# Stacked rounded queries and doubled keys for the attention scores of a two-block transformer kernel, with row sums from a column of ones

## The reference

```python
def _sliding_window_branch(q, k, v, z, sinks):
    ...
    s = jnp.einsum("bnqkgd,bnskd->bnkgqs", q, kb).astype(jnp.float32) * (SW_HD ** -0.5)
    s = jnp.where(valid[None, :, None, None], s, NEG_INF)
    ...
    p = jax.nn.softmax(jnp.concatenate([s, sink], axis=-1), axis=-1)[..., :-1]
    o = jnp.einsum("bnkgqs,bnskd->bnqkgd", p.astype(vb.dtype), vb).reshape(B, T, BRANCH_W)
    return o * jax.nn.silu(z)

def nsa_mixer(h, rel_bias, w_in, ...):
    ...   # o_cmp: attention over 15 compressed blocks
    o_sel = selected_attention(q, k_s, v_s, sel_idx, tbl, scale)   # here all 4 blocks are selected
    o_win = window_attention(q, k_w, v_w, tbl, scale)              # window 512 covers all 256 tokens
    o = gates[..., 0:1] * o_cmp + gates[..., 1:2] * o_sel + gates[..., 2:3] * o_win
    return o.reshape(B, S, H * NSA_V) @ w_o
```

## Time and profile before

| | |
|---|---|
| device time, median of 3 runs | 1417.76 us (1417.66 to 1418.02) |
| span of the profiled execution | 1415.6 us |
| median less the profiled span | 2.2 us |
| TensorE busy | 1403.6 us, 99% |
| VectorE, ScalarE, GpSimd busy | 924.5, 741.6, 65.1 us |
| share of TensorE in the chain that ended last | 94% |
| granted TensorE clock, mean | 0.999 |

### The profile page before, as it was taken

The page is one execution under the profiler, slowest core; times in us unless marked ns, Lnnn a source line. Parts: engine busy times, 40 slices in busy tenths (PEclk is TensorE's granted clock), DMA queues, the critical chain, the costliest instruction groups (busy, mean ns, idle before and its releaser), DMA issues.

```text
span 1415.6 us, 23050 instructions
## 1 busy us (share of the span) xinstructions
PE 1403.6 (99%) x8944; PEld 1270.0 (90%) x8944; DVE 924.5 (65%) x1341; ACT 741.6 (52%) x1008; POOL 65.1 (5%) x89
## 2 busy tenths in 40 slices
PE   9999999999999999999999999999999999999998
PEld 8989999999988888899888888888889999888886
DVE  5555797675566665777766666656657578666656
ACT  7556664343455445558554445544445358554454
POOL 2000010000010000010220000100000000200000
PEclk9999999999999999999999999999999999999999
DMA  8544431265545555561465554755555400555552
GB/s 325 189 146 143 168 131 60 90 209 193 179 155 201 180 197 186 174 200 59 163 260 196 187 191 166 260 186 178 188 197 184 144 31 2 185 210 184 194 191 89
DMA packets 34774, 239.69 MB, mean 169 GB/s; under 512 B 3914, under 2 KB 4058, under 8 KB 6928
## 3 DMA queue, kind: packets, MB, share of 16 engines
q1 hardware_dynamic: 32832, 231.39, 47.1%
q0 software_dynamic: 1440, 6.67, 1.5%
q10 hardware_dynamic: 432, 0.66, 0.1%
HBM read 237.10 MB, written 1.08 MB: 168 GB/s over the span
## 4 chain that ended last, share of the span: by engine, by line
PE 94%; DVE 2%; issue 1%; ACT 1%; DMA 0%; POOL 0%; POOLq 0%; ACTq 0%; DVEq 0%
PE ps L729 22%; PE ps L699 15%; PE ps L701 15%; PE ps L700 15%; PE ps L737 11%; PE ps L956 3%; PE ps L979 2%; PE ps L966 1%; PE ps L1243 1%; PE ps L2776 1%; PE ps L2784 1%; PE ps L638 1%; PE ps L2788 1%; PE ps L2952 1%; PE ps L820 1%
## 5 line engine op out<-in xcount | busy, mean ns | idle before, releaser
L406 DVE TENSOR_TENSOR low<-raw,high 128x2048 fp32r<-128x2048 f32 (+2 forms) x194 | 439.8, 2269 | 206.4 <-ACT high L400 203.9
L400 ACT ACTIVATE high<-raw 128x2048 fp32r<-128x2048 f32 (+1 forms) x197 | 372.1, 1891 | 44.8 <-PE ps L701 40.4
L729 PE MATMUL ps<-nt,high 128*128 128x512 f32 x1344 | 320.1, 390 | 0.0
L729 PEld LDWEIGHTS ps<-nt,high 128*128 128x128 f32 x1344 | 249.0, 188 | 50.7 <-issue 0.9
L699 PE MATMUL ps<-nt,high 128*128 128x256 f32 x656 | 186.0, 284 | 0.0
L701 PE MATMUL ps<-nt,low 128*128 128x256 f32 x656 | 184.8, 282 | 0.0
L700 PE MATMUL ps<-nt,high 128*128 128x256 f32 x656 | 184.8, 282 | 0.0
L737 PEld LDWEIGHTS ps<-nt,low 128*128 128x128 f32 x1344 | 167.5, 189 | 3.6
L737 PE MATMUL ps<-nt,low 128*128 128x256 f32 x1344 | 168.6, 283 | 0.0
L699 PE MATMUL ps<-high,hth 128*128 128x512 f32 x320 | 124.5, 389 | 0.0
L700 PE MATMUL ps<-low,hth 128*128 128x512 f32 x320 | 124.5, 389 | 0.0
(11 more groups left out here) (404 smaller groups left out, 2188.7 us busy)
## 6 DMA issues: line engine op xcount, KB each, us to landing
raw<-in_stream SPq DMA_DIRECT2D x215, 1024.0 KB, 4.9
late<-in_w POOLq DMA_DIRECT2D x1, 2048.0 KB, 9.4
scr<-bias_by_distance POOLq DMA_DIRECT2D x1, 2048.0 KB, 12.9
scr<-in_mem SPq DMA_DIRECT2D x2, 512.0 KB, 5.2
raw<-in_stream SPq DMA_DIRECT2D x4, 256.0 KB, 6.0
raw<-in_stream SPq DMA_DIRECT2D x2, 512.0 KB, 7.5
x<-in_x SPq DMA_DIRECT2D x1, 1024.0 KB, 8.0
con<-in_con SPq DMA_DIRECT2D x1, 592.0 KB, 8.9
```

What stands on the lines that cost most here:

```text
L400: nc.scalar.activation(high_of(t, slice(0, n)), raw[t % SLOTS][:, 0:n], ACT.Copy).then_inc(w_high, 1)
L406: nc.vector.tensor_tensor(low_of(t, slice(0, n)), raw[t % SLOTS][:, 0:n], high_of(t, slice(0, n)).bitcast(F32), ALU.subtract).then_inc(w_l ...
L729: last = nc.tensor.matmul(r3(bank, 2), w[:, k, P * j:P * j + P], nt[:, :, k, :], start=first and k == 0, stop=not first and k == KC - 1, s ...
```

## The change: what it does

**Scores of SW and NSA.** Each head's queries are stored twice over the partitions in one fp32r tensor: rounded on the 64 partitions where the head lies, the remainder on the other 64. The keys are stored on both halves, once rounded and once as remainder. One matmul over all 128 partitions then sums rounded query x key and remainder x key; the scores are two fp32r products (rounded keys, remainder keys) for each of the two token tiles, all 256 wide (L1011), in the place of f32 products 256 and 128 wide. MLA and XM keep their f32 scores. The zero-padded keys and their memsets go.

**Row sums.** The values get a 65th column of ones (a 129th for XM), so that L979's place (L1037 in the changed file) gives the row sum in PSUM. exp no longer accumulates, the mask instruction yields the scaled negative maximum directly, so the small instruction for it is gone in causal units.

**Outputs by two heads.** Reciprocal, gate and evacuation are one instruction each for two heads (256 columns). The loops run one iteration longer, and the turns of the outputs come one iteration later. The multiplication of the SW outputs by silu(z) and the addition of the NSA outputs into `late` move to GpSimd (4 and 16 instructions of 128x256), which raises `at_weighted`; `pe_turn("yc")` and the NSA turns wait for that.

**New preparation.** ScalarE makes the rounded queries and keys, VectorE the remainders; TensorE waits for `ns_low` 6 (all queries, ks and kw) ahead of NSA's first scores. Some buffers are placed elsewhere and some semaphores are merged.

The core of the diff:

```diff
+        def act_high_queries(q, j, src):
+            for own, _, heads in halves_of_heads(q, j):
+                last = nc.scalar.activation(heads[own], r3(src, 2)[own], ACT.Copy)
+            return last
+        def dve_low_queries(q, j, src):
+            for own, other, heads in halves_of_heads(q, j):
+                last = nc.vector.tensor_tensor(heads[other], r3(src, 2)[own], heads[own].bitcast(F32), ALU.subtract)
+            return last
+        def dve_low_keys(keys, n, src):
+            for (own, to, k), (_, _, high_) in zip(key_parts(keys[1], n), key_parts(keys[0], n)):
+                last = nc.vector.tensor_tensor(k[to], src[own], high_[own].bitcast(F32), ALU.subtract)
+            return last
...
+                products = u["products"]
                 for t in (1, 0):
-                    c = cols_of(u, t)
-                    last = nc.tensor.matmul(ps[a % 2][:, c], u["q"][:, P * t:P * t + P],
-                                            u["k"][:, 0:c.stop - c.start], start=True, stop=True)
+                    c = cols_of(u, t) if len(products) == 1 else slice(S - S * t, 2 * S - S * t)
+                    for n, (q, k) in enumerate(products):
+                        last = nc.tensor.matmul(ps[a % 2][:, c], q[:, P * t:P * t + P], k[:, 0:c.stop - c.start],
+                                                start=n == 0, stop=n == len(products) - 1, skip_group_check=True)
...
+                scale = q_negscale[:, t:t + 1] if u["scale"] is None else -u["scale"]
+                most = neg_sink[:, a - SW0:a - SW0 + 1] if sinks else 3e38
+                last = nc.vector.tensor_tensor_reduce(at_s[b][:, c], ps[a % 2][:, c], m, scale, most, ALU.add, ALU.min,
+                                                      at_nm[r][:, t:t + 1])
...
-            dve_step(dve, "swkv")
-            b = read_bank(dve, "swkv")
-            zeroed_here(dve, "sw_k")
-            for kv in range(SW_KV):
-                for half in range(2):
-                    nc.vector.tensor_copy(padded(sw["k"], kv, half)[64 * half:64 * half + 64],
-                                          b[64 * kv:64 * kv + 64, 0:S])
-            bank_read("swkv", nc.vector.tensor_copy(sw_vt, b[:, S:2 * S]))
             dve_turn(dve, "ym")
+            dve.wait_ge(sw_high, 3)
+            bank_read("swkv", dve_low_keys(sw_ks, SW_KV, r3(ps[bank_of("swkv")][:, 0:S], 1)))
...
             act_turn(act, "ym")
+            bank = read_bank(act, "swkv")
+            nc.scalar.activation(sw_vt, bank[:, S:2 * S], ACT.Copy)
+            act_high_keys(sw_ks, SW_KV, r3(bank[:, 0:S], 1)).then_inc(sw_high, 1)
...
+            for p in range(SW_H // 2):
+                pool.wait_ge(at_read, SW0 + 2 * p + 2)
+                yo, zo = (pair_of_heads(as3(b, TT), 2 * p, SW_D) for b in (sw["y"], sw["z"]))
+                nc.gpsimd.tensor_tensor(yo, yo, zo, ALU.mult).then_inc(at_weighted, 1)
...
+            for q in range(NSA_H):
+                pool.wait_ge(at_read, NSA0 + 2 * q + 2)
+                if q >= NSA_H // 2:
+                    pool.wait_ge(at_weighted, SW_H // 2 + q - NSA_H // 2 + 1)
+                yo = pair_of_heads(ny, 2 * q % NSA_H, NSA_D)
+                nc.gpsimd.tensor_tensor(yo, yo, ns_new(q), ALU.add).then_inc(at_weighted, 1)
...
-            pe.wait_ge(at_read, SW0 + SW_H)
+            pe.wait_ge(at_weighted, SW_H // 2)
             pe_turn(pe, "yc")
...
+            pe.wait_ge(ns_low, 6)
+            zeroed_here(pe, "nsa_ones")
```

More of the change, by code:

```diff
@@ new lines, in build, with stacked, high_low_keys @@
+        ml_v_ = [with_ones(v, 0, MLA_H, MLA_V) for v in (mls["v0"], ml["v1"])]
+        ns_v = {n: [with_ones(ns[n], t, NSA_G, NSA_D) for t in range(TT)] for n in ("vs", "vw")}
+        def stacked(q, heads):
+            return q.rearrange("p (h s) -> p h s", h=heads)
+        def high_low_keys(k, groups):
+            return [r3(k[:, S * groups * n:S * groups * n + S * groups], groups) for n in range(2)]
+        sw_qs, ns_qs = stacked(sw_queries, SW_H), stacked(ns_queries, NSA_H)
+        sw_ks = high_low_keys(sw_keys, SW_KV)
@@ L1083, in dve_units @@
                 if a < first + n:
+                    dve_scores(dve, ch, a, False)
+                ch.join()
+                if a < first + n:
+                    nc.vector.tensor_scalar(at_nm[a % RING], at_mx[a % RING], -UNITS[a]["scale"], None, ALU.mult)\
+                        .then_inc(at_max, 1)
+                if e >= first:
+                    evac(e, o, inv).then_inc(at_read, 1)
+        def dve_units(dve, ch, first, n, evac, lead, sinks=False, y=None, weigh=None, splits=()):
+            for a in range(first, first + n + 5):
+                if a == first + 2:
+                    lead()
+                p, odd = divmod(a - 4, 2)
+                ready = odd and first <= a - 4 < first + n
+                if ready:
+                    inv = at_inv[p % 3]
+                    dve.wait_ge(at_out, 2 * p + 2)
+                    sums = pair_out(p)[:, :, :, 64]
@@ L1091, in dve_units @@
-                    ins.then_inc(at_max, 1)
-                b, off = divmod(a - (first + n - 2 * KC) - 10, 4)
+                        ch.mark(nc.vector.tensor_tensor(by_unit(at_sums[p % 3]), sums, by_unit(at_sinkexp[p % 3]), ALU.add))
+                    else:
+                        ch.mark(nc.vector.reciprocal(by_unit(inv), sums))
+                if a < first + n:
+                    dve_scores(dve, ch, a, sinks)
+                if ready and sinks:
+                    ch.join()
+                    ch.mark(nc.vector.reciprocal(inv, at_sums[p % 3]))
+                elif ready and weigh:
+                    ch.join()
+                    ch.mark(weigh(p, inv))
@@ L1735, in _ @@
             ch.link(nc.gpsimd.memset(one_col, 1.0))
+            for v in xm_v + sw_v_:
+                last = nc.gpsimd.memset(v[:, :, v.shape[2] - 1:v.shape[2]], 1.0)
+            last.then_inc(zeroed, 1)
             pool.wait_ge(ident_here, 16)
@@ L2676, in _ @@
             pe_pair_tile(pe, "swz0", 1)
-            for name in ("swq0", "swq1"):
+            for name in ("swq0", "swq1", "swkv"):
                 wait_bank(pe, name)
-            pe.wait_ge(sw_v, 1)
+            pe.wait_ge(sw_high, 4)
             pe.wait_ge(turn_low, turn_done("ym"))
@@ L2917, in _ @@
             pe.wait_ge(ml_krd, 16)
+            zeroed_here(pe, "mla_ones")
             def rest_of_v():
```

395 lines of the change are left out of this document (226 added, 169 removed).

## The result

The changed kernel takes 1419.64 us in the median of 15 runs (1418.69 to 1421.83); the kernel before, run beside it, 1417.66 us (1417.40 to 1418.36). The ratio is 1.0015, 95% interval 1.0008 to 1.0021: slower by 0.15%, 2.0 us, where 1.0 us faster was forecast. The time lies inside the forecast's range and inside the 0.2% that the forecast takes as no change, but the interval excludes 1, and the sign is the opposite one. The profiled execution took 1419.13 us with a span of 1417.3, which is 1.7 more than the span of the kernel before (1415.6).

What follows compares the result with a forecast made beforehand. TensorE, busy 99% of the span, was taken to bound the kernel. The terms -7.0 + 3.7 + 1.4 + 2.4 - 1.5 = -1.0 us gave span 1414.6 and time 1416.7 against 1417.76, range 1413.4 to 1420.3.

Steps and rivals of the forecast that it cites:

- The start of NSA, +3.7 (3.0 to 3.7): Ahead of NSA's first scores TensorE idles 3.0 to 3.7 us, waiting for all of `ns_low`; 3.7 taken.
- rival (4): TensorE's clock starts slow after the stop at NSA's start, costing 1.9 to 3.0 us: 1418.6 to 1419.7; chance 0.13.
- Scores, -7.0: In 40 SW and NSA units four fp32r products take 0.176 us less than the f32 ones: -7.0 us.
- The claim that VectorE stays covered: In the SW and NSA units VectorE and ScalarE lose work, so stay covered though the unit shrinks to 1.47 us.
- the 65th column costs nothing: In the units, values growing from 64 to 65 columns are costed at nothing; 0.6 us if it cost its share.
- The way into SW, +1.4 (0.9 to 1.8): At swz0's second half TensorE waits for the bank of swkv, read late by VectorE's key remainders: 0.9 to 1.8 us.
- The end of SW, +2.4: At `pe_turn("yc")` GpSimd's silu(z) multiplication ends behind VectorE's split, turn 2.2 to 2.7 us late; about 0.5 if GpSimd starts first.
- The ends of the loops, -1.5: Three loop ends each lose 0.6 to 0.7 us to exp and evacuation; three quarters of 3 x 0.67 saved.
- GpSimd's NSA additions at nothing: In the NSA loop a sum of 256 columns has 1.2 us and needs 0.54 to 0.88, so costs nothing.
- rival (3): GpSimd's additions are too slow and each NSA turn waits: +2.9 at 1.85 us a sum, +5.6 at 2.3; chance 0.10.
- Rival (5): In the units fp32r scores run at 0.217 us each and don't become cheaper: +8.7 us, 1432.4; chance 0.03.
- From span to time, +2.2: Around the whole kernel's span lie 2.2 us (median less span), added to the forecast span to give the time.

Runs made afterwards that it cites:

- warm: The changed kernel with 8 extra f32 matmuls of 256 columns on TensorE ahead of the wait for the kw keys at NSA's start; 1417.58 us.
- all3_f32: all3 with the SW and NSA scores back as one f32 product per token tile, without the keys' remainders; 1415.71 us.
- all3: The changed kernel with kw keys waited for later, swkv's bank copied to SBUF first, and the last silu(z) multiplication on VectorE ahead of the split; 1409.98 us.
- split_waits: The changed kernel with VectorE waiting for GpSimd's last silu(z) multiplication ahead of the weight tile's split at the end of SW; 1416.96 us.
- keys_later: The changed kernel with TensorE's wait for the kw keys moved from NSA's first scores to ahead of the first values; 1413.63 us.
- bank_copied: The changed kernel with the bank of swkv copied early to SBUF by VectorE, rounded keys and remainders made from the copy; 1419.11 us.
- narrow: The changed kernel with the scores of token tile 0 128 columns wide in the place of 256; 1418.96 us.

## Why the prediction was wrong

The step that failed is the sum itself, which took TensorE's idle time as the whole price of a stop. "The start of NSA, +3.7 (3.0 to 3.7)" was right for the idle stretch (3.78 measured), and left out the slow products behind it: 1.46 us in the profile, up to 3.2 in those of other variants, 2.1 us between the medians of the changed kernel and warm. The mechanism stood beside the sum as rival (4), with a chance of 0.13 and a price of 1.9 to 3.0 taken from the slow start of the kernel; it came true. Those rows were the only ones in the trace of before with TensorE's work behind a long idle time (later it never idles over 0.64 us at once), and they did show what follows it. They deserved a term, not a doubt. The forecast span is 2.7 us short of the measured one; this accounts for 1.5 of them, the slower refilling of TensorE behind the stop for 0.3, the first 12 us for 0.5, and the items below for the rest.

The rest, by its own steps:

- **Scores, -7.0:** right for the 32 NSA units, 1.65 to 1.48 us each, and 5.5 us lost when all3_f32 undoes them. For the 8 SW units the size came out by luck: their stretch is 1.4 shorter, but in all3 only 0.3 of it hangs on the cheaper scores. The claim that VectorE stays covered failed there. That the 65th column costs nothing was right.
- **The way into SW, +1.4 (0.9 to 1.8):** measured 1.7. ScalarE's four keys took 1.55 and VectorE's remainders 1.73, both at the slow ends.
- **The end of SW, +2.4:** measured 2.6, with GpSimd's 2.70 us row behind the split, as forecast, and split_waits showed the reason. The Trainium skill's rule ("SBUF — State Buffer", "Who interferes with whom") holds here: the split was first by 0.16 us, and in split_waits GpSimd was first and took 0.73. What the step lacked is the slow clock that this stop also brings in some executions.
- **The ends of the loops, -1.5:** measured about -1.6, but as 0.9 at MLA and 0.66 at NSA; some 0.2 at SW were lost again to the longer stops at the masks. They are not three equal parts.
- **GpSimd's NSA additions at nothing:** right. They take 0.73 us each, no NSA turn waits for them, and rival (3) falls. Its argument for, that GpSimd took 2.1 to 2.6 us wherever VectorE split a weight, was read too widely: in the trace of before, L574 took 0.71 us at 416.65, with a split that began 0.56 us behind it. Rival (5) falls with the first row of the unit.
- **From span to time, +2.2:** 1.8 in every run of the changed kernel and of the kernel before that has a span listed; the 2.2 set the median of three runs against the span of another. With 1.8 the same sum gives 1416.4. (1414.6 + 2.2 is 1416.8, not 1416.7.)
- **The range:** 1413.4 to 1420.3 held the time, because rival (4) reached into it.

With the profile's sizes the sum is -7.0 + 4.0 (idle and refilling) + 1.7 + 2.6 - 1.6 + 1.5 + 0.5 = +1.7, the measured difference of the spans. The 1.5 is the slow clock and the 0.5 the first 12 us, which the change doesn't touch.

## What to carry to other kernels

Where TensorE is busy 99% of the time, price a stop like those here (2.0 to 3.8 us) as the stop plus what the clock loses behind it, which was between nothing and 3.2 us, and look in the trace for the first work after its longest idle stretch to size that; before taking a stop as given, look whether its wait can stand at the first use of what it guards, since here that one line was worth 6.0 us. Repairs of single stops can look worthless while another stop remains whose after-effect comes and goes, so judge them together, and read the spread of the runs as well as the median. Work handed to GpSimd on the critical path needs the order against VectorE's instructions with two SBUF inputs checked, not only its own duration.

## What was not expected of the hardware

A stop of 2.35 us at the same instruction was followed by full clock in three profiles (changed, keys_later and warm, 1.00 over 120 to 140 us) and by the slow one in two others (bank_copied, where 1.5 us were lost, and narrow, 0.91), and after a stop of 2.02 us two of 11 runs were 2 us longer than the rest. Behind one and the same stop of 3.78 us, between 5 and 21 weight products ran slowly. Busy work of no use in a stop, 16 instructions of f32 products, made the kernel 2.1 us faster. Of the two neighbouring fp32r products of 128 columns in a unit, the first started its successor after 0.06 us and the second after 0.11, so the unit gained 0.04 us and not 0.12; that the loads of the weights hold the second was not tested. The first 12 us varied by up to 0.9 us between profiles with the same instructions of TensorE, by where the slow start ended.
